# Second block's prelude: the compression weights in the idle half of h, position rows between weight loads, and other orders on four engines

## The chip, the cores and the metric

The kernel is one program on one core of a Trainium2 chip. The metric is the device time of one launch in microseconds. The time before is 1586.78 us, the median of three runs (1584.68 to 1588.28).

## The reference, cut to what matters

The program computes four layers over 256 latent and 256 context tokens (width 1024), and then one block of another kind over the 256 latent tokens. The change lies where the second begins. There, `h` is the normed latent activation and `w_in` one wide projection. Only its first mixer has the compression:

```python
h = rms_norm(x, norm_mix[l])
cols = split_columns(h @ w_in[l])          # a_q a_kc a_vc a_ks a_vs a_kw a_vw a_gate b_* c_* merge
def compress(z, which):                    # z = a_kc or a_vc, windows of 32 tokens, stride 16: 15 of them
    blk = z[:, :, win_idx] + cmp_pos[which]
    hid = jax.nn.gelu(blk.reshape(b, G, n_cmp, CMP_LEN * HEAD_DIM) @ cmp_w1[which])
    return hid @ cmp_w2[which]
k_cmp = rms_norm(compress(kc, 0), k_g)
v_cmp = compress(vc, 1)
bias_c = jnp.transpose(tab[t5_bucket(dist_c)], (2, 3, 0, 1))     # relative position bias, 16 heads
logits_c = jnp.einsum('bgrtd,bgnd->bgrtn', q, k_cmp) * scale + bias_c
```

`cmp_w1` is two matrices of 2048 x 256. The three attention branches (compressed, selected and windowed in the first mixer, one band in the second, a causal one with forgetting in the third) make 80 score units of 128 queries each. A merge and a gated MLP follow.

## The kernel before, in words

Everything is FP32. A product with a weight is done as three fp32r matmuls: ScalarE copies a raw piece of 128 x 512 into a high part (`act_cast`, `s_whi`), VectorE makes the rest (`dve_cast`, `s_wlo`), TensorE multiplies high by high, low by high and high by low. The activation is held in two such halves too, `Hh` and `Hl`, each [128, 8, 512]: columns 0 to 255 are the context's, 256 to 511 the latent tokens'. After the fourth layer's keys and values nobody reads the context's columns again.

SyncE loads the weights in the order of one list of jobs (`plan`, `sp_loads`), 512 KB a chunk, into a ring of four chunks (`s_raw`). A chunk waits until the chunk four before it is cast (or, for weights used raw in FP32, multiplied). SyncE's queue is in order, so a waiting load holds all behind it. The jobs of `cmp_w1` are ("w1", which, half), two chunks each. They are used raw: `pe_hid` multiplies a half by the windows `ST` in 8 small matmuls, and both halves sum up in bank 1. The result goes through `act_hid` part 0 (a copy into the tile `OS`), `pe_hid_sum` (a matmul with a selection matrix), `act_hid` part 1 (GELU into `HID`) and `pe_hid_out`. For the keys (`which` 0) come a norm (`v_hid_k`, a square on ScalarE, `v_hid_mean`, `POOL`, `v_hid_n`), a transpose (`pe_hid_turn`) and the scaled copy `KC`, which the first score unit needs. The values end in `VM`.

The position bias is 16 strips of 128 KB, read from a small DRAM tensor `ext_rows` with overlapping rows, one DMA a head.

The order of work in the second block is written out by hand, one function an engine: `pe_second`, `act_second`, `v_second`, `sp_all`. The prelude does the first six products of 256 columns (`pe_product_2` with keys 512, 768, 1024, 0, 256, 1816, each for two blocks of tokens i = 0, 1), the head norms and turns, and the compression. A head's norm is `act_take` (bank to `NQ` in `s_X`), `act_head_sq`, `v_head_mean`, a power on GpSimd, `v_head_n`, `pe_head_turn` and `act_head_ev`. Then 86 slots follow. A slot of TensorE has about two chunks (three matmuls each) of the remaining products, a transpose of probabilities (`pe_prob`) of the unit four slots before, and one score. VectorE's slot s has the row maximum of unit s - 1 (`v_row_max_2`), the normalisation of unit s - 3 and up to two casts. Up to unit 8 a score also waits for the row maximum of the unit before it.

Of the kernel before, what the change touches and what calls it, by code (L numbers as in the profile page):

```python
# [237 lines left out]
def plan_2():  # L238
# [21 lines left out]

def plan():
# [108 lines left out]
class Weights:  # L370


    def __init__(self, jobs, dram, areas, hi, lo, placed, spent):
# [11 lines left out]
        for j in jobs:  # L385
# [43 lines left out]
class Net:  # L429

    def __init__(self, nc, ctx, ins, out):
        self.nc, self.ins, self.out = nc, ins, out
# [37 lines left out]
        self.w = Weights(jobs, ins["weights"], {0: raw, 1: self.SF[:, 0:8192], 2: GF[:, :]}, hi, lo, placed, self.spent)  # L470
        self.cast = {"act": 0, "dve": 0}

# [2420 lines left out]
    def pe_hid_sum(self, pe, w):  # L2893
        pe.wait_ge("hid_a", (1, 5)[w])
# [3 lines left out]
        for q in range(2):  # L2898
            mk = pe.matmul(self.ps[w][:, 64 * q:64 * q + 64], self.tile_2("OS")[:, 128 * q:128 * q + 128], self.tile_2("selC"), start=True, stop=True)
# [45 lines left out]
    def pe_second(self, pe):  # L2945
# [32 lines left out]
        self.pe_hid_sum(pe, 1)  # L2978
# [916 lines left out]
```

## Time and profile before

| | us |
|---|---|
| median of three runs | 1586.78 |
| the profiled execution | 1587.17 |
| its span | 1585.4 |
| TensorE busy | 1512.4 |
| VectorE busy | 1009.7 |
| ScalarE busy | 808.1 |
| idle of TensorE in 1100 to 1120 us | 5.07 |

The profiled execution lasted 1.8 us longer than its span (what lies around the first and last instruction). The prelude that the change rewrites runs from about 1060 to 1113 us, the slots from there to about 1280 us. A timeline row is: start, length (both us), engine, line, operation, destination and source, shapes, count of instructions merged, and in brackets the idle time before it and what ended it. A `x16` row of `s_raw,s_X` is one `pe_hid` (each FP32 matmul is recorded as two).

### The profile page before, as it was taken

The numbers are of one execution on the slowest core, as the hardware profiler recorded it, in microseconds if no ns is written. First come the engines' busy times: TensorE is split into PE (matmuls) and PEld (weight loads), VectorE is DVE, ScalarE is ACT, GpSimd is POOL, SyncE is SP. The second block draws the span as 40 slices with busy tenths as digits, with TensorE's granted clock in tenths as the row PEclk, the third lists the DMA queues.
The fourth block names the chain that finished last, engine by engine and source line by source line (L and its number), as shares of the span: only waits on it lengthen the run. The fifth ranks groups of instructions, "written<-read, shape, count | busy, mean of one in ns | idle before, by whom it ended". The sixth has DMA issues, their size and how long they took to land.

```text
span 1585.4 us, 28886 instructions
## 1 busy us (share of the span) xinstructions
PE 1512.4 (95%) x11163; PEld 1310.3 (83%) x11163; DVE 1009.7 (64%) x2579; ACT 808.1 (51%) x1956; POOL 110.4 (7%) x220
## 2 busy tenths in 40 slices
PE   6999999999999988999999999888999999999998
PEld 4777779977889967888999888787777799999997
DVE  3687775655555555676676699665566565566655
ACT  3565664544444444333334566655666444465543
POOL 1011110100000110010001111001101000000000
PEclk9999999999999999999999999999999999999999
DMA  9543322334322322232222442237322245555563
GB/s 362 222 121 108 99 76 88 150 103 128 113 93 90 130 94 93 92 111 104 94 94 81 176 119 83 78 120 244 116 79 62 77 130 177 173 186 160 197 198 111
DMA packets 59963, 203.41 MB, mean 128 GB/s; under 512 B 7731, under 2 KB 10499, under 8 KB 59826
## 3 DMA queue, kind: packets, MB, share of 16 engines
q1 hardware_dynamic: 58081, 197.08, 36.5%
q0 software_dynamic: 1600, 4.28, 1.4%
q8 instruction: 89, 1.46, 0.4%
q14 instruction: 49, 0.39, 0.1%
q10 hardware_dynamic: 144, 0.20, 0.0%
HBM read 200.43 MB, written 1.07 MB: 127 GB/s over the span
## 4 chain that ended last, share of the span: by engine, by line
PE 78%; DVE 11%; ACT 4%; issue 3%; DMA 2%; SPq 1%; POOL 1%; DVEq 0%; ACTq 0%
PE ps L48 74%; PE ps L51 5%; DVE s_wlo L57 2%; ACT SF L54 2%; DVE SF L60 1%; DVE SF L66 1%; SPq L87 1%; DVE SF L57 1%; DVE s_SR L57 1%; DVE SF L75 1%; ACT s_whi L54 1%; DMA s_raw<-in_weights_dram 1%; DMA SF<-in_weights_dram 1%; DMA SF<-in_mlmask_dram 1%; DVE s_G L57 1%
## 5 line engine op out<-in xcount | busy, mean ns | idle before, releaser
L57 DVE TENSOR_TENSOR s_wlo<-s_raw,s_whi 128x512 fp32r<-128x512 f32 (+1 forms) x490 | 317.0, 682 | 120.4 <-ACT s_whi L54 119.2
L48 PE MATMUL ps<-s_Hh,s_whi 128*128 128x256 f32 (+2 forms) x992 | 324.0, 327 | 8.9 <-DVE s_Hl L57 8.0
L48 PE MATMUL ps<-s_Hh,s_wlo 128*128 128x256 f32 (+2 forms) x992 | 312.7, 315 | 0.0
L48 PE MATMUL ps<-s_Hl,s_whi 128*128 128x256 f32 (+2 forms) x992 | 312.5, 315 | 0.0
L54 ACT ACTIVATE s_whi<-s_raw 128x512 fp32r<-128x512 f32 (+1 forms) x490 | 281.5, 620 | 54.5 <-PE ps L48 50.0
L54 ACT ACTIVATE SF<-ps 128x512 f32<-128x512 f32 (+3 forms) x328 | 146.6, 463 | 259.8 <-PE ps L51 170.8
L48 PEld LDWEIGHTS ps<-s_Hh,s_whi 128*128 128x128 f32 (+1 forms) x992 | 188.4, 190 | 36.2 <-issue 16.9
L48 PE MATMUL ps<-s_whi,s_Hh 128*128 128x256 f32 (+1 forms) x688 | 209.0, 304 | 6.2 <-DVE s_wlo L57 5.5
L48 PEld LDWEIGHTS ps<-s_Hh,s_wlo 128*128 128x128 f32 (+1 forms) x992 | 188.7, 190 | 13.1
L48 PE MATMUL ps<-SF 128*64 128x128 f32 (+6 forms) x1368 | 192.4, 313 | 6.5 <-DVE SF L60 4.2
L48 PEld LDWEIGHTS ps<-s_Hl,s_whi 128*128 128x128 f32 (+1 forms) x992 | 189.0, 190 | 10.7
L48 PE MATMUL ps<-s_wlo,s_Hh 128*128 128x256 f32 (+1 forms) x688 | 195.4, 284 | 0.0
L48 PE MATMUL ps<-s_whi,s_Hl 128*128 128x256 f32 (+1 forms) x688 | 195.3, 284 | 0.0
L48 PEld LDWEIGHTS ps<-SF 128*64 128x64 f32 (+2 forms) x1368 | 125.3, 158 | 56.4 <-issue 36.9
L48 PEld LDWEIGHTS ps<-s_whi,s_Hh 128*128 128x128 f32 x688 | 132.7, 193 | 17.7 <-issue 8.5
L51 PE MATMUL ps<-s_K,SF 128*128 128x128 f32 (+5 forms) x780 | 128.1, 276 | 17.7 <-DVE SF L60 7.4
L48 PEld LDWEIGHTS ps<-s_wlo,s_Hh 128*128 128x128 f32 x688 | 132.8, 193 | 0.8
L48 PEld LDWEIGHTS ps<-s_whi,s_Hl 128*128 128x128 f32 x688 | 132.6, 193 | 0.0
L54 ACT ACTIVATE SF<-SF,s_st 128x513 f32<-128x513 f32 (+5 forms) x208 | 115.2, 554 | 21.0 <-DVE s_st L75 14.5
L51 PEld LDWEIGHTS ps<-s_K,SF 128*128 128x128 f32 (+5 forms) x780 | 93.3, 142 | 31.8 <-DVE SF L60 11.0
L57 POOL TENSOR_TENSOR s_st<-s_st,s_mhalf 128x1 f32<-128x1 f32 (+4 forms) x58 | 55.7, 961 | 785.2 <-DVE s_st L60 785.1
L48 PE MATMUL ps<-s_whi,s_Gh 128*128 128x256 f32 x336 | 99.0, 295 | 7.8 <-DVE s_Gl L57 6.1
(198 smaller groups left out, 2571.2 us busy)
## 6 DMA issues: line engine op xcount, KB each, us to landing
s_raw<-in_weights_dram SPq DMA_DIRECT2D x308, 512.0 KB, 4.1
GF<-in_weights_dram SPq DMA_DIRECT2D x32, 512.0 KB, 9.0
SF<-in_weights_dram SPq DMA_DIRECT2D x16, 512.0 KB, 13.3
s_raw<-in_weights_dram SPq DMA_DIRECT2D x6, 384.0 KB, 3.4
s_gp<-in_l_g_post_dram POOLq DMA_DIRECT2D x16, 128.0 KB, 3.8
s_bg<-in_l_b_ada_dram POOLq DMA_DIRECT2D x16, 128.0 KB, 4.5
SF<-ext_rows SPq DMA_DIRECT2D x16, 128.0 KB, 3.1
s_X<-in_ctx_dram SPq DMA_DIRECT2D x2, 512.0 KB, 5.2
```

The source lines that it names most:

```text
L48: return self.e.matmul(*a, **k)
L51: return self.e.transpose(*a, **k)
L54: return self.e.activation(*a, **k)
L57: return self.e.tensor_tensor(*a, **k)
L60: return self.e.tensor_scalar(*a, **k)
L66: return self.e.scalar_tensor_tensor(*a, **k)
L75: return self.e.tensor_tensor_reduce(*a, **k)
L87: return self.e.dma_start(*a, **k)
```

## The change

The four `w1` jobs no longer go through the ring. They have a place of their own, `HF`, an FP32 view of the context's columns of `Hh` and `Hl`. Those of the keys stand in the load list ahead of the fourth layer's `w_out`; those of the values come into the same places once the keys' halves are multiplied. Half of the 16 strips are loaded with a load between every two, the other half after the first row maximum. On TensorE, ScalarE and VectorE the steps stand in another order, and the values' `OS` has a tile of its own, `OS1`.

```diff
+        lone = {("w1", w, h): self.w1_place(w, h) for w in range(2) for h in range(2)}
+    def w1_place(self, w, h):
+        tile = self.HF[:, h]
+        free = ("v_mm", V_AT[3] + 2) if w == 0 else ("w1", h + 1)
+        return lambda c: (tile[:, c.k0:c.k1, 0:256], f"area{4 * h + c.k0 // 4}", 3 + w, free)
...
-    jobs = [p(512), p(768), p(1024), small, p(0), w1(0, 0), p(256), w1(0, 1), w1(1, 0), p(1816), w1(1, 1)]
+    jobs = [p(512), p(768), p(1024), small, p(0), p(256), p(1816), w1(1, 0), w1(1, 1)]
...
-        jobs += mix(l) + [job(("out", l, j), f"l{l}_w_out", 256 * j, 256) for j in range(4)]
+        jobs += mix(l) + (first_w1() if l == 3 else []) + [job(("out", l, j), f"l{l}_w_out", 256 * j, 256) for j in range(4)]
@@ def pe_second
         self.pe_hid(pe, 0, 0)
+        self.pe_hid(pe, 0, 1)
         self.pe_head_turn(pe, 0)
         pe.wait_ge("p_ev", 2)
         self.pe_product_2(pe, ("p", 256), 4, 0, range(8), 6)
         self.pe_small_sums(pe)
         self.pe_head_turn(pe, 1)
-        self.pe_hid(pe, 0, 1)
+        self.pe_hid_sum(pe, 0)
         self.pe_product_2(pe, ("p", 256), 4, 1, range(8), 6)
-        self.pe_hid_sum(pe, 0)
+        self.pe_hid(pe, 1, 0)
+        self.pe_hid_out(pe, 0)
         self.pe_head_turn(pe, 2)
-        self.pe_hid(pe, 1, 0)
         pe.wait_ge("p_ev", 4)
         self.pe_product_2(pe, ("p", 1816), 5, 0, range(8), 7)
-        self.pe_hid_out(pe, 0)
+        self.pe_hid(pe, 1, 1)
         self.pe_head_turn(pe, 3)
-        self.pe_hid(pe, 1, 1)
         self.pe_product_2(pe, ("p", 1816), 5, 1, range(8), 7)
+        self.pe_hid_sum(pe, 1)
         self.pe_hid_turn(pe)
-        self.pe_hid_sum(pe, 1)
@@ def act_second
         self.act_take(act, 0, 7)
+        self.act_hid(act, 0, 0)
         self.act_head_ev(act, 0)
         self.act_head_sq(act, 2)
         self.act_head_ev(act, 1)
-        self.act_hid(act, 0, 0)
+        self.act_hid(act, 0, 1)
+        self.act_take(act, 256, 6)
+        self.act_cast(act, w.first(("p", 1816)) + 2)
+        self.act_head_sq(act, 3)
         cast(("p", 1816))
-        self.act_take(act, 256, 6)
-        self.act_hid(act, 0, 1)
-        self.act_head_sq(act, 3)
         self.act_head_ev(act, 2)
+        self.act_hid(act, 1, 0)
@@ def v_second
         cast(("p", 1304))
+        v.wait_ge("ld_strip", 128)
         self.v_head_mean(v, 4)
+        self.v_row_max_2(v, 0)
         self.v_head_n(v, 4)
-        v.wait_ge("ld_strip", 256)
...
-            self.dve_cast(v, self.castable(at, at + 2, **self.slot_done(slot)))
+            if slot > 1:
+                self.dve_cast(v, self.castable(at, at + 2 + 2 * (slot < 4), **self.slot_done(slot)))
@@ def sp_all
-        self.sp_loads(sp, self.load_at(("p", 0)))
+        self.sp_loads(sp, self.load_at(("p", 1816)))
         sp.wait_ge("st_ext", 16)
         sp.wait_ge("turned", 40)
         sp.wait_ge("p_mm", 1)
         for h in range(16):
+            if h == 8:
+                self.sp_loads(sp, self.load_at(("p", ORDER_2[3])))
+                sp.wait_ge("row_max", UNIT_AT[4] + 1)
             src = bass.AP(ext.tensor, ext.offset + 384 * h + 1, [[1, 128], [1, 256]])
             sp.dma_start(self.F(7424, 16, 256)[:, h, :], src).then_inc(S["ld_strip"], 16)
+            if h % 2 == 1:
+                self.sp_loads(sp, self.loaded + 1)
```

SyncE's queue from the first step of the prelude. `SF<-ext_rows` is a strip, `HF` a `w1` chunk, `s_raw` a chunk of the ring; before the change:

```order
L87 DMA s_raw<-in_weights_dram 128x1024 x6
L87 DMA s_raw<-in_weights_dram 128x256
L87 DMA s_raw<-in_weights_dram 128x1024 x2
L87 DMA SF<-ext_rows 128x256 x16
L87 DMA s_raw<-in_weights_dram 128x1024 x138
```

and with it:

```order
L87 DMA s_raw<-in_weights_dram 128x1024 x6
L87 DMA s_raw<-in_weights_dram 128x256
L87 DMA s_raw<-in_weights_dram 128x1024 x6
L87 DMA SF<-ext_rows 128x256 x2
L87 DMA HF<-in_weights_dram 128x4x256
L87 DMA SF<-ext_rows 128x256 x2
L87 DMA HF<-in_weights_dram 128x4x256
L87 DMA SF<-ext_rows 128x256 x2
L87 DMA HF<-in_weights_dram 128x4x256
L87 DMA SF<-ext_rows 128x256 x2
L87 DMA HF<-in_weights_dram 128x4x256
L87 DMA s_raw<-in_weights_dram 128x1024 x8
```

The chunks of products 256 and 1816 now stand ahead of the strips; the values' `w1` stands between them.

ScalarE in the middle of the prelude: `s_X<-ps` is `act_take`, `s_gp<-ps` the copy into `OS`, `s_CS<-ps` the GELU, `s_whi<-s_raw` casts of 1816. Before:

```order
L54 ACTIVATE SF<-ps,s_VC 128x512
L54 ACTIVATE s_gp<-ps 128x256
L54 ACTIVATE s_whi<-s_raw 128x512 x4
L54 ACTIVATE s_X<-ps 128x512
L54 ACT_TABLE_LOAD
L54 ACTIVATE s_CS<-ps 128x128
L54 ACTIVATE SF<-s_X 128x512
L54 ACTIVATE SF<-ps,s_VC 128x512
```

and with the change:

```order
L54 ACTIVATE SF<-ps,s_VC 128x512
L54 ACT_TABLE_LOAD
L54 ACTIVATE s_CS<-ps 128x128
L54 ACTIVATE s_X<-ps 128x512
L54 ACTIVATE s_whi<-s_raw 128x512 x2
L54 ACTIVATE SF<-s_X 128x512
L54 ACTIVATE s_whi<-s_raw 128x512 x2
L54 ACTIVATE SF<-ps,s_VC 128x512
```

The GELU and its table now stand ahead of product 256's take and of the casts, and the square of head 3 (`SF<-s_X`) between the second and the third cast.

VectorE where the slots begin (`L75` is a row maximum, `s_G` head 4's norm, `s_wlo` casts of product 1560):

```order
+L75 ISA SF,s_st<-ps,SF 128x7
+L75 ISA s_st 128x1
 L57 TENSOR_TENSOR s_G<-s_X,s_st 128x4x64 x2
-L57 TENSOR_TENSOR s_wlo<-s_raw,s_whi 128x512 x2
 L75 ISA SF,s_st<-ps,SF 128x7
 L75 ISA s_st 128x1
-L57 TENSOR_TENSOR s_wlo<-s_raw,s_whi 128x512 x2
-L75 ISA SF,s_st<-ps,SF 128x7
-L75 ISA s_st 128x1
+L57 TENSOR_TENSOR s_wlo<-s_raw,s_whi 128x512 x4
```

The first row maximum stands ahead of head 4's norm, and the four casts between the second and the third maximum instead of two and two from the start.

## Rows read from the trace of the kernel before

**Rows 1.** Windows of 20 us: busy us (count) by engine, PE clock, DMA share, GB/s.
```profile
1080.00:1100.00 20.00, 18.22 (x168) 14.79 (x167) 9.22 (x23) 11.44 (x21) 2.65 (x2) 1.00 0.73 258
1100.00:1120.00 20.00, 14.93 (x97) 11.84 (x97) 10.07 (x31) 10.49 (x26) 3.33 (x3) 0.76 0.63 227
1120.00:1140.00 20.00, 20.00 (x135) 15.52 (x135) 11.49 (x51) 10.98 (x38) 2.01 (x1) 0.99 0.17 54
```

**Rows 2.** Timeline of TensorE, its waits and marks from 1082 to 1123 us.
```profile
1082.09 1.40 PE L48 MATMUL ps<-s_raw,s_X 128*32 128x256 f32 x16
...
1085.56 0.35 PE L48 MATMUL ps<-s_Gh,s_Hh 128*128 128x256 f32 x1 [1.48 <-DVE s_Gl L57]
...
1103.83 1.11 PE L51 MATMUL ps<-s_K,s_X 128*128 128x128 f32 x4 [3.24 <-DVE s_X L57]
...
1111.61 0.66 PE L48 MATMUL ps<-s_K,s_gp 128*128 128x64 f32 x4 [1.43 <-ACT s_gp L54]
...
1112.96 0.38 PE L48 MATMUL ps<-s_band,SF 64*128 64x7 f32 x2
...
1114.96 0.59 PE L48 MATMUL ps<-s_band,SF 64*128 64x7 f32 x2 [0.40 <-DVE s_st L75]
...
1122.47 0.27 PE L51 MATMUL ps<-s_K,SF 128*7 128x128 f32 x1
```

**Rows 3.** Timelines of ScalarE, VectorE and GpSimd, 1079 to 1115 us.
```profile
1079.14 0.21 ACT L54 ACTIVATE adaF<-ps 128x48 f32<-128x48 f32 x1 [2.14 <-PE ps L51]
...
1084.06 2.39 ACT L54 ACTIVATE s_Gh<-s_raw 128x512 fp32r<-128x512 f32 x4 [4.71 <-DMA s_raw<-in_weights_dram]
...
1098.32 1.28 ACT L54 ACT_TABLE_LOAD   x1
1099.61 0.28 ACT L54 ACTIVATE s_CS<-ps 128x128 f32<-128x128 f32 x1
...
1101.41 1.64 POOL L57 TENSOR_TENSOR s_st<-s_st,s_mhalf 128x8 f32<-128x8 f32 x1 [8.37 <-DVE s_st L60]
...
1103.08 0.69 DVE L57 TENSOR_TENSOR s_X<-s_X,s_st 128x512 f32<-128x512 f32 x1 [1.57 <-POOL s_st L57]
...
1113.53 1.29 DVE L57 TENSOR_TENSOR s_wlo<-s_raw,s_whi 128x512 fp32r<-128x512 f32 x2
```

**Rows 4.** Windows of 1 us in which the granted clock changes, columns as in rows 1.
```profile
1103.00:1104.00 1.00, 0.17 (x1) 0.17 (x2) 0.89 (x3) 0.00 (x0) 0.05 (x1) 0.75 0.53 213
...
1106.00:1107.00 1.00, 1.00 (x9) 0.26 (x2) 0.78 (x2) 1.00 (x3) 0.00 (x0) 0.54 0.00 0
...
1113.00:1114.00 1.00, 1.00 (x8) 0.98 (x8) 1.00 (x3) 1.00 (x3) 0.00 (x0) 0.87 0.65 266
...
1120.00:1121.00 1.00, 1.00 (x7) 0.86 (x6) 0.00 (x0) 0.61 (x1) 0.00 (x0) 0.72 0.08 20
```

**Rows 5.** Timeline of TensorE: how long the pieces last at either clock.
```profile
1088.38 0.28 PE L48 MATMUL ps<-s_Gh,s_Hl 128*128 128x256 f32 x1
...
1090.18 0.66 PE L51 MATMUL ps<-s_K,s_G 128*128 128x128 f32 x4
1090.77 1.07 PE L48 MATMUL ps<-s_raw,s_X 128*32 128x256 f32 x16
...
1099.95 0.63 PE L48 MATMUL ps<-s_gp,s_CS 128*32 128x64 f32 x8
...
1104.87 1.94 PE L48 MATMUL ps<-s_raw,s_X 128*32 128x256 f32 x16
...
1115.48 1.06 PE L48 MATMUL ps<-s_gp,s_CS 128*32 128x64 f32 x8
```

**Rows 6.** Who PE waited for, 1121 to 1282 us: total us, times, longest.
```profile
PE ps L51 <- DVE SF L60: 0.8, 2, 0.5
```

**Rows 7.** Windows of 1 us: strips alone in flight, then weight chunks alone.
```profile
1074.00:1075.00 1.00, 1.00 (x11) 0.95 (x10) 0.29 (x4) 0.00 (x0) 0.80 (x1) 1.00 0.93 256
...
1080.00:1081.00 1.00, 1.00 (x11) 1.00 (x10) 0.74 (x5) 0.00 (x0) 0.00 (x0) 1.00 0.99 406
```

More of the change, by code:

```diff
@@ L130, in raw @@
         c = self.chunk(k)
+        if len(c.raw.shape) == 3:
+            return c.raw[:, k - c.k0, :]
         return c.raw[:, (k - c.k0) * self.w:(k - c.k0 + 1) * self.w]
@@ L258, in plan_2, with w1, first_w1 @@
     return jobs
+def w1(w, h):
+    return Job(("w1", w, h), [(0, "cmp_w1_2", (0, w), 1024 * h, 0, 256)], 8, 256, False)
+def first_w1():
+    return [w1(0, 0), w1(0, 1)]
 def plan():
@@ L390, in __init__ @@
             for c in j.chunks:
+                if j.key in lone:
+                    c.raw, c.sem, c.nth, c.before = lone[j.key](c)
+                    cols = (c.k1 - c.k0) * j.w
+                    c.off, off = off, off + 128 * cols
+                    c.src = dram[c.off:off].rearrange("(p k c) -> p k c", p=128, c=j.w)
+                    continue
                 mine, n = rings[j.ring], areas[j.ring].shape[1] // CHUNK
@@ L434, in __init__ @@
         self.X = sb("X", [128, 4, D])
+        with nc.sbuf_tensor("HF", [128, 2, 8, 512], F32) as self.HF:
+            pass
         self.Hh, self.Hl = sb("Hh", [128, 8, 512], R32), sb("Hl", [128, 8, 512], R32)
@@ L469, in __init__ @@
         self.ada_last = {j.key: n + 1 for n, j in enumerate(j for j in jobs if j.key[0] == "ada")}
[L470 removed]
+        lone = {("w1", w, h): self.w1_place(w, h) for w in range(2) for h in range(2)}
+        self.w = Weights(jobs, ins["weights"], {0: raw, 1: self.SF[:, 0:8192], 2: GF[:, :]}, hi, lo, placed, lone, self.spent)
         self.cast = {"act": 0, "dve": 0}
+    def w1_place(self, w, h):
+        tile = self.HF[:, h]
+        free = ("v_mm", V_AT[3] + 2) if w == 0 else ("w1", h + 1)
+        return lambda c: (tile[:, c.k0:c.k1, 0:256], f"area{4 * h + c.k0 // 4}", 3 + w, free)
     def F(self, at, *shape):
@@ L2761, in tile_2 @@
             return a[:, at:at + (48 if name == "GS" else 16)].rearrange("p (i g) -> p i g", i=2)
+        if name == "OS1":
+            return self.bg[:, 0, :]
         if name in ("OS", "W2"):
@@ L2898, in pe_hid_sum @@
         for q in range(2):
-            mk = pe.matmul(self.ps[w][:, 64 * q:64 * q + 64], self.tile_2("OS")[:, 128 * q:128 * q + 128], self.tile_2("selC"), start=True, stop=True)
+            mk = pe.matmul(self.ps[w][:, 64 * q:64 * q + 64], self.tile_2("OS" if w == 0 else "OS1")[:, 128 * q:128 * q + 128], self.tile_2("selC"), start=True, stop=True)
         mk.then_inc(self.S["hid_pe"], 1)
@@ L3253, in act_hid @@
             if w == 1:
-                act.wait_ge("hid_v", 2)
-            act.activation(self.tile_2("OS"), self.ps[1][:, 0:256], ACT.Copy).then_inc(S["hid_a"], 1)
+                act.wait_ge("gate_g", 16)
+            act.activation(self.tile_2("OS" if w == 0 else "OS1"), self.ps[1][:, 0:256], ACT.Copy).then_inc(S["hid_a"], 1)
         else:
-            act.wait_ge("hid_pe", 1 if w == 0 else 4)
+            act.wait_ge("hid_pe", 1 if w == 0 else 3)
             act.activation(self.tile_2("HID"), self.ps[w][:, 0:128].rearrange("p (c m) -> p c m", c=2), ACT.Gelu_apprx_tanh).then_inc(S["hid_a"], 1)
@@ L3550, in v_second @@
         self.v_head_n(v, 3)
-        mean = self.v_hid_mean(v)
-        self.v_hid_n(v, mean)
+        self.v_hid_n(v, self.v_hid_mean(v))
         cast(("p", 1304))
+        v.wait_ge("ld_strip", 128)
         self.v_head_mean(v, 4)
+        self.v_row_max_2(v, 0)
         self.v_head_n(v, 4)
-        v.wait_ge("ld_strip", 256)
         for slot in range(SLOTS_2 + 1):
             u = slot - 1
-            if 0 <= u < 80:
+            if 0 < u < 80:
                 self.v_row_max_2(v, u)
@@ L3592, in v_row_max_2 @@
             mask = strip[:, 8 * br + h, 128 - 128 * i:256]
+        if br == 1:
+            v.wait_ge("ld_strip", 256)
         if u > 3:
```

16 lines of the change are left out of this document (7 added, 9 removed).

## The prediction

> **What bounds the kernel now.** I first read the windows of 20 us. TensorE is busy for nearly all of 1120 to 1140 us, but only 14.93 us of the 20 between 1100 and 1120, where its granted clock is 0.76 as well, and 18.22 between 1080 and 1100 [rows 1]. Then TensorE's timeline through the prelude. It has three long waits: 1.48 us for VectorE's cast of product 256, 3.24 us for head 2's norm, 1.43 us for the values' copy `OS`, and 0.40 us at the second score [rows 2]. Third, the other engines, to see what lies behind those waits. ScalarE casts product 256 only at 1084.06, after 4.71 us for a weight DMA [rows 3]; that chunk is queued behind all 16 strips. Fourth, the list of waits in the slots: the largest entry there is 0.8 us in 160 us [rows 6], so from the first slot on TensorE's own work sets the pace, and what it gains before them reaches the end. Last, the windows of 1 us for the clock.
>
> **What the old stretch consists of.** My marks are the first `pe_hid` at 1082.09, the first score at 1112.96 and the first transpose of probabilities at 1122.47 [rows 2]; the change alters nothing on TensorE outside them.
> From 1082.09 to 1112.96 are 30.87 us. The waits are 1.48 + 3.24 + 1.43 = 6.15, and 0.33 more in the first `pe_hid`, which takes 1.40 where one undisturbed takes 1.07 [rows 2, 5]. Two very small waits of about 0.2 each I leave in. In the windows of 1 us the clock is at half (1.2 instead of 2.4 GHz) from about 1103.5 to 1106.9: 0.75 in the first window means a half of it slow, 0.54 in the last 0.92 [rows 4]. What ran there is four transposes (1.11 against 0.66), a `pe_hid` (1.94 against 1.07) [rows 2, 5]: 0.45 + 0.87 = 1.3 us. Work at full clock: 30.87 - 6.15 - 0.33 - 1.3 = 23.1, and without the two small waits 22.7.
> From 1112.96 to 1122.47 are 9.51 us. One wait of 0.40; the clock is at half again from about 1113.74 to 1120.56 [rows 4]. `pe_hid_out` takes 1.06 there against 0.63, the transposes 0.45 more. An estimate for the rest: half of the remaining 4 or 5 us that run slow. I take 2.8 in all. Work at full clock 6.3.
>
> **Removed and moved on SyncE.** With the change the six loads up to product 1816 stand ahead of the strips. The chunks of 256 wait only for casts of earlier products, so they land well before ScalarE, free at 1079.35 [rows 3], wants them; it casts them until 1081.8 and VectorE until 1083.4. The 1.48 is gone; next after it is nothing until head 0's turn. The keys' `w1` is loaded 100 us earlier, so 0.33 goes too. Those four chunks (2 MB) come ahead of the fourth layer's `w_out`. The DMA queues are idle more than half of the time there, and the ring is four chunks deep, so I cost them at nothing; if that cover were gone, each of the four would hold `w_out` by 2 us.
> Now the new wait: the values' first `w1` chunk waits in SyncE's queue until TensorE has multiplied the keys' first half, at 1083.2 by the walk below. Behind it are six strips, three `w1` chunks and product 1304's two chunks, 3.93 MB. Chunks into `HF` are cut in pieces of 1 KB a row, as the strips are. Strips alone moved 256 GB/s, ring chunks alone 406 [rows 7]. I take the strips' rate for `HF`: 2.88 MB / 0.256 = 11.3 us, then 1.05 / 0.406 = 2.6, and about 1.5 until the last has landed: 1098.6. ScalarE wants 1304 at 1100.1. It fits, by little. The Trainium skill, DMA: Bandwidth & Descriptors, Specifications, says that pieces of 512 B and more reach the line rate. The rows here speak against it for 1 KB pieces (256 against 406). By the page these loads would land by 1094.5 and the rival on them below would have no chance; the sum stays as it is.
>
> **The walk with the new orders**, each step by the lengths above (product 2.94 a block, from 1085.56 to 1088.38 and 0.12 [rows 2, 5]). TensorE: two `pe_hid` to 1084.2, turn of head 0 1084.8, product 256 block 0 1087.8, small sums 1089.3, turn 1 1089.9, `pe_hid_sum` 1090.3, block 1 1093.2, `pe_hid` of the values 1094.3, `pe_hid_out` 1094.9. Turn 2 needs head 2's norm. Its square is no more behind four casts, a take and a table load: done 1086.4, mean, power 1.64 and multiply 0.69 [rows 3] give 1090.4. So the 3.24 is gone. Turn 2 ends at 1095.5.
> Product 1816 needs its casts. ScalarE: table load 1.28 and GELU from 1090.4 to 1092.1, take of 256 at 1093.2 (it waits for TensorE), two casts to 1094.9, square of head 3, two casts to 1096.6. VectorE's first low part is ready at 1095.1, each next in time. Block 0 ends at 1098.4, second `pe_hid` of the values at 1099.5. Turn 3 is what comes late next: VectorE has all four low parts at 1097.3, then the mean (0.9), the power (1.64) and the multiply (0.69): 1100.6. A new wait of 1.1 us stands here. Behind it on TensorE: the block 1 of 1816, and with it everything.
> Turn 3 to 1101.2, block 1 to 1104.1, `pe_hid_sum` and `pe_hid_turn` to 1104.8, two chunks to 1105.5. `KC` is ready at 1105.1 (the copy `OS1` is made at 1099.8 in a tile of its own, so the 1.43 goes). The first score stands at 1105.5. By the other sum, 1082.09 + 22.7 + 1.1 = 1105.9. I take 1105.7: 7.3 us earlier.
> The Trainium skill, ScalarE: Activation LUTs, What ACT_TABLE_LOAD costs, adds a drain of 1.38 us to each load of 1.28. The rows show the load of 1.28 with the GELU 0.01 us behind it [rows 3], so the sum has no drain. By the page the casts of 1816 would come 1.4 us later and TensorE would wait about 1 us more.
>
> **At the start of the slots.** The 0.40 goes, since the first row maximum now stands ahead of head 4's norm. But four casts (2 x 1.29 [rows 3]) stand ahead of the third row maximum, for which score 3 waits: VectorE does row maximum 1 at 1108.4, the casts to 1110.9, row maximum 2 to 1111.2, and TensorE is there at 1110.2. A new wait of 1.0. The slow clock before was preceded by 3.24 + 1.43 us without work and a time of small instructions; with waits of 1.1 and 1.0 I expect full speed. Gain 2.8 + 0.4 - 1.0 = 2.2.
>
> **Sum.** 7.3 + 2.2 = 9.5, and as all the many handovers are taken without slack, I take off 0.3: 9.2 us. From the profiled execution, 1587.17 - 9.2 = 1578.0; the median of three is 0.4 below that execution, so 1577.6. What happens from the first transpose on is unchanged, except half of the strips, which come with 30 to 70 us to spare before unit 48.
> Bounds: the clock's 4.1 us (1.3 + 2.8) may not come back at all, which leaves 5.1. On the good side, the two new waits (2.1) may be shorter or hidden, and the later slow spells in the slots may vanish: 12 at most.
>
> **The rivals.** *A slow spell stays.* TensorE still does many small FP32 matmuls and transposes and has two waits. Then 2.8 to 4.1 are missing: 1581. For it: the spell at 1113.7 came only 1.43 us of wait after 7 us at full clock [rows 2, 4]. Against: that stretch had two waits, the new one has the same sum in smaller parts. *Loads come late.* At 200 GB/s for `HF` and strips, the last lands at 1101.7, at 160 at 1105.3, 5.2 us after ScalarE wants it; ScalarE has 1.2 to spare, so 4.0 lost: 1581.6. *The stall only moves.* If the turns and norms, not the loads, are what TensorE really waits for, the 3.24 comes back at turn 3: 9.2 - 3 - 2 (its slow clock) gives 1582. *Slower.* SyncE's queue behind the keys' `w1`: if pieces of 1 KB of weights move at 100 GB/s (4 times as many descriptors as a ring chunk), 28.8 + 2.6 + 2 us bring 1304 to 1116.6, 16.5 after it is wanted, 15.3 of them on the path: 1577.6 + 15.3 = 1593. It decides below about 130 GB/s, where 9.2 + 1.2 us of delay are used up. The strips at 256 speak against it. *It doesn't do what it says:* if the slots, not the prelude, set the end, 1586.8. Rows 6 speak against it.
>
> **How the numbers follow.** Forecast 57% (its own range 1575 to 1580); slow spell 17%; loads late 7%; the stall moves 8%; no change 6%; slower 5%. The range to 1583 holds the first four cases and down to 1574 the better end. No change means within 0.2%, 3.2 us, about what this measurement can tell. Faster by more: 57 + 17 + 7 + 6 of the 8 = 0.87; same 0.08; slower 0.05.
>
> **What would show it.** In the profile after: product 256 without a wait; no wait over 0.5 at turn 2; a wait of about 1 at turn 3 and at score 3; the first score near 1105.7 and the first transpose of probabilities near 1113; clock 1.00 from 1100 to 1120; SyncE's issues of the values' `w1` at 1083 and later. I am wrong if ScalarE waits for a DMA at product 1304, if the clock has a spell of 0.5 there, or if the distance from the first transpose to the end is more than 1 us longer than before (462.9 us to the end of the span, 1585.4 - 1122.47).

## The result, and the profile after

The change makes the kernel faster: 1578.58 us, the median of seven runs (1574.91 to 1581.33), against 1586.51 (1583.12 to 1594.13) for the kernel before on the same chip. The ratio is 0.9942, with a 95% interval of 0.9923 to 0.9961, so 9.2 us with an interval of 6.2 to 12.2. Forecast were 1577.6 us and 9.2 us. The profiled execution of after lasted 1574.91 us (span 1573.1). It is the fastest of the seven, so its 12.3 us below the profiled one of before say too much.

The windows of 20 us of after, columns as in [rows 1]:

```profile
1080.00:1100.00 20.00, 18.84 (x191) 15.87 (x190) 10.67 (x28) 12.59 (x25) 4.28 (x3) 1.00 0.77 247
1100.00:1120.00 20.00, 19.61 (x144) 16.52 (x143) 12.54 (x49) 13.94 (x41) 1.69 (x2) 1.00 0.37 123
```

The second window is the one to compare: 19.61 us of TensorE at full clock, where before it was 14.93 at 0.76. The timeline of TensorE after answers to [rows 2]:

```profile
1081.88 1.93 PE L48 MATMUL ps<-HF,s_X 128*32 128x256 f32 x32
...
1084.15 0.36 PE L48 MATMUL ps<-s_Gh,s_Hh 128*128 128x256 f32 x1
...
1093.85 0.66 PE L51 MATMUL ps<-s_K,s_X 128*128 128x128 f32 x4
...
1099.82 0.66 PE L51 MATMUL ps<-s_K,s_X 128*128 128x128 f32 x4 [1.16 <-DVE s_X L57]
...
1104.82 0.38 PE L48 MATMUL ps<-s_band,SF 64*128 64x7 f32 x2
...
1109.99 0.48 PE L48 MATMUL ps<-SF 64*128 64x128 f32 x2 [0.39 <-DVE s_st L75]
...
1111.58 0.27 PE L51 MATMUL ps<-s_K,SF 128*7 128x128 f32 x1
```

From the top: both `pe_hid` of the keys in one piece, product 256 without a wait, turn 2 without a wait, turn 3 with 1.16, the first score, score 3 with 0.39, the first transpose of probabilities. Of 6.55 us of waits at four places, 1.55 at two places are left. The turn behind the 3.24 of before was turn 3 as well, not turn 2 as the prediction has it (below). The engines behind the waits, after, as in [rows 3]:

```profile
1079.03 2.18 ACT L54 ACTIVATE s_Gh<-s_raw 128x512 fp32r<-128x512 f32 x4
...
1089.91 1.28 ACT L54 ACT_TABLE_LOAD   x1
1091.21 0.28 ACT L54 ACTIVATE s_CS<-ps 128x128 f32<-128x128 f32 x1
...
1097.41 1.64 POOL L57 TENSOR_TENSOR s_st<-s_st,s_mhalf 128x8 f32<-128x8 f32 x1 [8.63 <-DVE s_st L60]
...
1107.24 2.49 DVE L57 TENSOR_TENSOR s_wlo<-s_raw,s_whi 128x512 fp32r<-128x512 f32 x4
```

ScalarE casts product 256 as soon as it is free, with no DMA wait in front (before 4.71). The power for head 3 runs from 1097.41, after all of VectorE's casts of 1816; that makes the 1.16. The four casts at 1107.24 make the 0.39. Two of the windows of 1 us, in which [rows 4] had 0.54 and 0.87:

```profile
1106.00:1107.00 1.00, 1.00 (x12) 0.86 (x11) 0.52 (x2) 0.98 (x3) 0.44 (x1) 1.00 0.97 360
...
1113.00:1114.00 1.00, 1.00 (x8) 0.67 (x6) 0.32 (x2) 0.65 (x3) 0.00 (x0) 1.00 0.79 247
```

All windows from 1096 to 1126 us show 1.00. Last, the waits of TensorE in the slots after, 1111 to 1274 us, which answer to [rows 6]:

```profile
PE ps L51 <- DVE SF L60: 0.8, 2, 0.5
PE ps L51 <- ACT SF L54: 0.3, 1, 0.3
```

**How the traces are compared.** The executions reach the first `pe_hid` between 1079.8 and 1087.3 us, whatever the kernel. So I count from there to the first score and to the first transpose of probabilities ("transpose" below). Each row of the table is one profiled execution. Half clock is the time at 1.2 instead of 2.4 GHz between 1080 and 1125 us, summed from windows of 1 us (a window at 0.75 counts as a half). The ratio is to the kernel before on the same chip.

| kernel | waits of TensorE, us | first score | transpose | half clock | ratio (95%) |
|---|---|---|---|---|---|
| before | 1.48, 3.24, 1.43, 0.40 | 30.87 | 40.38 | 3.4 + 6.8 | 1 |
| after | 1.16, 0.39 | 22.94 | 29.70 | 0 | 0.9942 (0.9923 to 0.9961) |
| after again, `c_after` | 1.15, 0.39 | 22.94 | 29.71 | 0 | 0.9918 (0.9892 to 0.9944) |
| `e1_old_pe_act` | 0.97, 1.44 | 24.70 | 33.94 | 6.8 | 0.9958 (0.9927 to 0.9989) |
| `e2_old_sp` | 1.15, 0.39 | 22.94 | 29.71 | 0 | 0.9915 (0.9883 to 0.9947) |
| `e3_shared_os` | 1.15, 1.29 | 24.35 | 35.05 | 10.2 | 0.9960 (0.9936 to 0.9985) |
| `e4_old_dve` | 1.16, 2.48 | 22.93 | 34.72 | 6.8 | 0.9965 (0.9938 to 0.9991) |
| `e5_delay` | 2.21, 0.39 | 24.00 | 30.77 | 0 | 0.9926 (0.9902 to 0.9951) |
| `e6_mean_early` | 0.25 | 22.17 | 28.48 | 0 | 0.9901 (0.9872 to 0.9930) |
| `e7_both` | 0.24 | 22.17 | 28.48 | 0 | 0.9910 (0.9884 to 0.9936) |
| `e8_keys_w1_late` | 1.15, 0.39 | 22.95 | 29.72 | 0 | 0.9940 (0.9918 to 0.9961) |
| `e9_delay_at_turn` | 0.25, 1.54, 0.38 | 24.19 | 33.40 | 6.8 | 0.9963 (0.9938 to 0.9989) |
| `e10_long_delay` | 4.20, 0.39 | 27.50 | 34.27 | 3.4 | 0.9955 (0.9937 to 0.9973) |
| `e11_os1_alone` | 1.20, 3.24, 1.02, 1.11 | 30.09 | 37.59 | 3.4 | 0.9988 (0.9971 to 1.0005) |

The distances repeat to 0.02 us where nothing is altered (after, `c_after`, `e2`, `e8`), while the intervals of the ratios are some 5 to 10 us wide. Steps of 1 us are read from the distances, and the ratio only tells that they reach the end. Where they are larger, the times bear them out: `e1` to `e4` ran on one chip, and the medians of `e1`, `e3` and `e4` lie 6.0, 4.6 and 5.0 us above that of `e2`, whose transpose stands where after's does; by the transposes it is 4.2, 5.3 and 5.0. No execution of `e3` or `e4` was as fast as the slowest of `e2`.

### The profile page after: what moved, and what is told of

Its sections match the earlier page's. It is cut to its first block, busy times and chain, and to the rows that moved or that the text cites. A ratio compares the mean times of both kernels' runs of the same rounds, so it can differ in the third digit from the quotient of the medians.

```text
span 1573.1 us, 28886 instructions
## 1 busy us (share of the span) xinstructions
PE 1505.4 (96%) x11163; PEld 1306.8 (83%) x11163; DVE 1008.6 (64%) x2579; ACT 807.7 (51%) x1956; POOL 110.2 (7%) x220
## 4 chain that ended last, share of the span: by engine, by line
PE 80%; DVE 11%; ACT 4%; issue 3%; DMA 1%; SPq 1%; POOL 1%; DVEq 0%; ACTq 0%
PE ps L48 75%; PE ps L51 5%; DVE s_wlo L57 2%; ACT SF L54 2%; DVE SF L60 1%; DVE SF L66 1%; DVE SF L57 1%; DVE s_SR L57 1%; DVE SF L75 1%; ACT s_whi L54 1%; DMA SF<-in_weights_dram 1%; DMA SF<-in_mlmask_dram 1%; SPq L87 1%; DVE s_G L57 1%; POOL s_st L57 1%
## 5 line engine op out<-in xcount | busy, mean ns | idle before, releaser
L48 PEld LDWEIGHTS ps<-s_Hl,s_whi 128*128 128x128 f32 (+1 forms) x992 | 188.5, 190 | 10.7
```

Of the source, the lines that this page charges most:

```text
L48: return self.e.matmul(*a, **k)
```

## The experiments

### Undoing one part at a time

**The orders of TensorE and ScalarE.** `e1` has the new loads and VectorE's new order, with the old `pe_second` and `act_second` and the shared `OS`. (It also undoes two exchanges on ScalarE that no run undoes alone: the casts of product 1304 ahead of head 3's copy, and `KC` ahead of head 4's square.)

```diff
-        self.pe_hid(pe, 0, 1)
         self.pe_head_turn(pe, 0)
...
+        self.pe_hid_turn(pe)
         self.pe_hid_sum(pe, 1)
-        self.pe_hid_turn(pe)
...
-        self.act_hid(act, 0, 0)
         self.act_head_ev(act, 0)
```

> The changed kernel with TensorE's and ScalarE's orders and the shared OS tile of before; loads (HF, strips) and VectorE's slots stay as changed. Theory A (the waits of before came from late weight loads, first of all): with the loads alone there is no wait at product 256, none at turn 2, about 0.5 us at turn 3, and the wait of about 1.4 us for the values' copy stays; first score near 1106.2 (changed kernel 1104.8, before 1113.0), clock full from 1100 to 1120, time about 1.4 us above the changed kernel's. Theory B (the orders of TensorE and ScalarE are worth as much as the loads): a wait of 2 us or more comes back at turn 2 or 3, first score at 1108.5 or later, time 4 us or more above the changed kernel's.

Measured: 1581.74 us (1576.6 to 1595.3). The wait of 1.48 does not come back, and where 3.24 stood there are 0.97, so the new orders of TensorE and ScalarE are not needed to shorten those two. What comes back is the wait for the values' copy and a stretch at half clock. Theory A was right on which waits stay (0.5 forecast at turn 3) and nearly on the first score (24.3 us after the first `pe_hid`), and wrong on the clock and so on the time. TensorE's timeline, and two windows, of `e1`:

```profile
1103.37 0.66 PE L51 MATMUL ps<-s_K,s_X 128*128 128x128 f32 x4 [0.97 <-DVE s_X L57]
...
1109.77 0.66 PE L48 MATMUL ps<-s_K,s_gp 128*128 128x64 f32 x4 [1.44 <-ACT s_gp L54]
```

```profile
1112.00:1113.00 1.00, 1.00 (x6) 0.79 (x4) 0.40 (x2) 0.98 (x3) 0.00 (x0) 0.50 0.00 0
...
1117.00:1118.00 1.00, 1.00 (x6) 1.00 (x7) 0.79 (x5) 0.51 (x3) 0.00 (x0) 0.50 0.89 320
```

**SyncE's order.** `e2` has all 16 strips ahead of product 256 again, and the values' `w1` behind them.

```diff
-        self.sp_loads(sp, self.load_at(("p", 1816)))
+        self.sp_loads(sp, self.load_at(("p", 0)))
...
-            if h == 8:
-                self.sp_loads(sp, self.load_at(("p", ORDER_2[3])))
-                sp.wait_ge("row_max", UNIT_AT[4] + 1)
...
-            if h % 2 == 1:
-                self.sp_loads(sp, self.loaded + 1)
```

> The changed kernel with SyncE's order of before in the prelude: all 16 strips in one go after product 0's chunks, then products 256 and 1816, then the values' w1 into HF. The keys' w1 stays early. Theory A: ScalarE waits about 4.7 us for product 256's chunk as before, TensorE waits 1.0 to 1.5 us at product 256; the rest of the new orders absorbs the delay (ScalarE's square of head 2 comes at about 1090.5, ahead of where turn 2 needs it), so first score near 1106.5, time about 2 us above the changed kernel's. Theory B (SyncE's order is the whole gain): the 3.2 us wait at turn 2 or 3 is back and a slow spell with it, first score near 1111, time 8 us above the changed kernel's.

Measured: 1575.78 us (1573.95 to 1577.3), distances equal to after's. ScalarE's timeline in `e2`:

```profile
1084.04 2.44 ACT L54 ACTIVATE s_Gh<-s_raw 128x512 fp32r<-128x512 f32 x4 [2.43 <-DMA s_raw<-in_weights_dram]
```

ScalarE waits 2.43 us for product 256's chunk, which lands 0.3 us ahead of the first `pe_hid` (before 2.0 behind it, since two chunks of the keys' `w1` were queued ahead of it too), and TensorE does not wait at all, since its two `pe_hid` (1.93 us) and the turn of head 0 lie ahead. Both theories fell. With the keys' `w1` out of the way, the strips' place is worth nothing.

**The keys' early `w1`**, the counterpart: `e8` loads it in the prelude, still into its own place.

```diff
-        jobs += mix(l) + (first_w1() if l == 3 else []) + [job(...)]
+        jobs += mix(l) + [job(...)]
...
-    jobs = [..., small, p(0), p(256), p(1816), w1(1, 0), w1(1, 1)]
+    jobs = [..., small, p(0), w1(0, 0), p(256), w1(0, 1), p(1816), w1(1, 0), w1(1, 1)]
```

> The changed kernel, but the keys' four w1 chunks are loaded in the prelude (the first half between products 0 and 256, the second between 256 and 1816), still into their own place, not the ring. All else as with the change. Theory (the early load of the keys' w1 is what takes the wait for product 256 away: 2 MB more now stand in SyncE's queue near it, and moved 400 GB/s they take 5 us): ScalarE's casts of 256 come up to 5 us later, TensorE waits 0.5 to 2 us at product 256 or at the first pe_hid; if that is all, the total is 1 to 2 us over the changed kernel. Rival (with the strips behind 1816 the queue has slack, so this too is worth nothing, like SyncE's order): the same as the changed kernel within 0.5 us. Second rival (the wait also brings a stretch at half clock): 4 to 6 us over.

Measured: 1576.95 us (1571.79 to 1580.22), again after's distances. ScalarE's cast of product 256 in `e8` has no wait for a DMA:

```profile
1084.42 2.18 ACT L54 ACTIVATE s_Gh<-s_raw 128x512 fp32r<-128x512 f32 x4
```

The rival held. The keys' `w1` ahead and the strips behind do the same job, and one of the two is enough. The two were not undone together with the rest kept. That the loads suffice for the 1.48 is shown by `e1`, where the old orders of TensorE and ScalarE stand with the new loads and product 256 has no wait. No run has the new orders with the old loads, so what the orders would save by themselves there, and at turn 3, is open.

**The values' own tile.** `e3` puts the copy back into the shared `OS`, behind `KC`.

```diff
-        self.pe_hid_sum(pe, 1)
         self.pe_hid_turn(pe)
+        self.pe_hid_sum(pe, 1)
...
-        self.act_hid(act, 1, 0)
...
+        self.act_hid(act, 1, 0)
         self.act_hid(act, 1, 1)
```

> The changed kernel with the values' copy again in the keys' OS tile, so after the keys' norm: the copy stands last of ScalarE's prelude and the selection matmul after the keys' turn. Theory A: TensorE waits 1.2 to 1.5 us between the keys' turn and that matmul, first score near 1106.2, time 1.4 us above the changed kernel's, and no slow spell. Rival: the wait brings the slow clock back within 5 us, as it did before, and costs 3 us more (4.5 in all).

Measured: 1580.33 us (1578.23 to 1583.47). TensorE's timeline and a window of `e3`:

```profile
1103.23 0.66 PE L48 MATMUL ps<-s_K,s_gp 128*128 128x64 f32 x4 [1.29 <-ACT s_gp L54]
```

```profile
1105.00:1106.00 1.00, 1.00 (x5) 1.00 (x5) 0.85 (x4) 1.00 (x3) 0.00 (x0) 0.50 0.79 311
```

The wait costs 1.41 us at the first score. From there to the transpose it takes 10.70 instead of 6.76, although after's wait of 0.39 is not there: 3.94 + 0.39 = 4.3 for the half clock. The rival was right in kind, with 4.3 where it had 3. `e1` undoes this part as well, and its transpose comes at 33.94, ahead of the 35.05 here. So beside `OS1` the new orders of TensorE and ScalarE bring 0.35 us at the first score (24.70 against 24.35) and nothing at the transpose; the 4.2 of `e1` is mostly the values' copy and the clock behind it.

**VectorE's order at the slots.** `e4` has head 4's multiply ahead of the first row maximum, and two casts in every slot from the first.

```diff
         self.v_head_mean(v, 4)
-        self.v_row_max_2(v, 0)
         self.v_head_n(v, 4)
...
-            if slot > 1:
-                self.dve_cast(v, self.castable(at, at + 2 + 2 * (slot < 4), ...))
+            self.dve_cast(v, self.castable(at, at + 2, ...))
```

> The changed kernel with VectorE's order of before where the slots begin: head 4's norm and two casts ahead of the first row maximum, two casts more ahead of the second. First score unchanged at 1104.8. Theory A: the first row maximum ends at 1108.6, so score 1 waits 2.5 us for it (0.39 at score 3 goes), first transpose of probabilities near 1113.7 instead of 1111.6, time 2 us above the changed kernel's. Rival: VectorE's order is hidden (before, the wait there was 0.40), time the same.

Measured: 1580.73 us (1578.85 to 1587.92). TensorE's timeline and a window of `e4`:

```profile
1110.72 0.39 PE L48 MATMUL ps<-s_band,SF 64*128 64x7 f32 x2 [2.48 <-DVE s_st L75]
```

```profile
1113.00:1114.00 1.00, 1.00 (x5) 0.55 (x4) 0.00 (x0) 0.00 (x0) 0.00 (x0) 0.50 0.75 287
```

From the first score to the transpose 11.79 us instead of 6.76: 5.03, of which 2.09 (2.48 - 0.39) are waits and 2.94 the half clock. Theory A had the wait (2.5) and not the clock.

### One part alone

`e11` is the kernel before with `OS1`, its early copy and the two steps of TensorE exchanged.

```diff
-        self.pe_hid_turn(pe)
         self.pe_hid_sum(pe, 1)
+        self.pe_hid_turn(pe)
...
+        self.act_hid(act, 1, 0)
         self.act_head_sq(act, 4)
-        act.wait_ge("hid_pe", 3)
+        act.wait_ge("hid_pe", 4)
...
-        self.act_hid(act, 1, 0)
```

> The kernel before with one part of the change alone: the values' copy has the tile OS1 and is made ahead of head 4's square, and pe_hid_sum of the values stands ahead of pe_hid_turn. The 1.43 us wait goes; the waits of 1.48 at product 256 and 3.24 at turn 2 stay. Theory (this wait and the clock's second fall behind it belong together): first score 1.4 earlier (29.4 us after the first pe_hid), first transpose of probabilities 1.4 + 2.8 earlier (36.2), total 4 us under the kernel before. Rival (the second fall came from the 3.24 us and the small matmuls before it): 1.4 us under, at 39.0. Second rival (the copy now stands ahead of head 4's square or KC and delays the first score): no gain.

Measured: 1585.69 us (1582.14 to 1589.42), 1.9 us by the ratio, with an interval that holds 0. TensorE's timeline and windows of `e11`:

```profile
1100.91 0.80 PE L51 MATMUL ps<-s_K,s_X 128*128 128x128 f32 x4 [3.24 <-DVE s_X L57]
...
1108.18 0.66 PE L48 MATMUL ps<-s_K,s_bg 128*128 128x64 f32 x4 [1.02 <-ACT s_bg L54]
...
1112.31 0.39 PE L48 MATMUL ps<-s_band,SF 64*128 64x7 f32 x2 [1.11 <-DVE s_st L75]
```

```profile
1102.00:1103.00 1.00, 1.00 (x16) 0.40 (x8) 0.74 (x5) 1.00 (x3) 0.00 (x0) 0.50 0.00 0
...
1113.00:1114.00 1.00, 1.00 (x11) 0.87 (x8) 0.54 (x3) 0.77 (x4) 0.00 (x0) 1.00 0.71 164
```

The theory was half right. The clock's second fall is gone, and from the first score to the transpose it takes 7.50 instead of 9.51, although a wait there is 0.71 longer: 2.7 us for that fall. But 1.02 of the 1.43 stays (`OS1` is ready late in the old order of ScalarE), and the gain goes into a new wait of 1.11 for a row maximum. The first fall, behind the 3.24, is untouched.

### What makes the clock fall

The runs above left two ideas: what counts is how long TensorE waits (S, the sum of its waits), or where (P, the place). Three kernels add waits, two of them to after and one to `e6` (below), by memsets of a free bank on VectorE, each waiting for the one before. `c_after` is the measure beside the first.

> The changed kernel itself, unaltered, as the measure for the three kernels beside it on this chip. Expected: 1578.6 us as before, ratio to the kernel before 0.994, within 0.15%; first score 22.9 us and first transpose of probabilities 29.7 us after the first pe_hid; no stretch at half clock between 1080 and 1125 us.

Measured: 1575.26 us (1571.28 to 1577.89). The distances came as expected, to 0.01 us. The ratio, 0.9918, is 0.0024 lower, beyond the 0.15% expected; the two intervals overlap.

```diff
         self.v_hid_k(v)
+        for _ in range(4):      # e5; 7 in e10
+            v.step(v.memset(self.ps[5][:, :], 0.0))
+            v.after()
         self.v_head_n(v, 3)
```

> The changed kernel with four extra memsets of a free bank of PSUM on VectorE, each waiting for the one before (about 0.6 us each, 2.5 in all), ahead of head 3's norm multiply. TensorE's wait at turn 3 then grows from 1.16 to about 3.7 us; nothing else is altered, and the output is the same. Theory (a wait of this length near the stretch of small FP32 matmuls is paid twice, once as the wait and once as a stretch at half clock behind it): a stretch of several us at half clock follows, first transpose of probabilities 29.7 + 2.5 + 3 to 4 = 35 to 36 us after the first pe_hid, total 5.5 to 6.5 us over the changed kernel. Rival (the clock falls for another reason, such as which small matmuls stand there, and a wait costs only its own length): 32.2 us, total 2.5 over, clock 1.00. Second rival (nothing, since VectorE has slack): same as the changed kernel; speaks against it that turn 3 waited for VectorE.

Measured: 1576.34 us (1575.37 to 1578.28), 1.1 over `c_after`. 1.57 us of the 2.67 of memsets lay in VectorE's own wait for GpSimd, so the wait at turn 3 grew by 1.06 only, from 1.15 to 2.21, and that is all it cost (1.06 at the transpose). The theory that a wait is always paid twice fell, for a wait of 2.21 at this place.

> The changed kernel with seven such memsets ahead of head 3's norm multiply instead of four. The wait at turn 3 was 1.16 + 4 x 0.67 - 1.57 = 2.21 (measured) with four, so it will be 4.2 to 4.3 with seven, longer than the 3.24 of the kernel before. Theory S (sum of waits): a stretch at half clock follows, first transpose of probabilities 29.7 + 3.1 + 2 to 4 = 35 to 37 us after the first pe_hid. Theory P (place: big matmuls stand behind this wait, the small ones come 4 us later): clock 1.00, 32.8 us.

Measured: 1580.46 us (1575.45 to 1581.82). TensorE's timeline and windows of `e10`:

```profile
1103.31 0.66 PE L51 MATMUL ps<-s_K,s_X 128*128 128x128 f32 x4 [4.20 <-DVE s_X L57]
```

```profile
1103.00:1104.00 1.00, 0.69 (x6) 0.69 (x7) 0.59 (x3) 0.00 (x0) 0.29 (x1) 0.92 0.00 0
1104.00:1105.00 1.00, 1.00 (x6) 1.00 (x6) 0.57 (x4) 0.69 (x1) 0.39 (x1) 0.50 0.00 0
...
1107.00:1108.00 1.00, 1.00 (x9) 1.00 (x9) 0.56 (x1) 0.00 (x0) 0.00 (x0) 0.87 0.71 115
```

3.05 us of wait more, and 3.4 us at half clock right behind, which cost 4.56 - 3.05 = 1.5. Then full clock again.

`e9` is `e6` (below) with a wait that ends 1.6 us ahead of the first score:

```diff
         v.wait_ge("rs", mean)
+        for _ in range(4):
+            v.step(v.memset(self.ps[5][:, :], 0.0))
+            v.after()
         for g in range(2):
```

> On the better version (head 3's mean early, no wait at turn 3), four memsets of a free bank of PSUM, each waiting for the one before (0.67 us each), stand ahead of the multiply of the compressed keys, so that TensorE waits 1.5 to 1.9 us at pe_hid_turn, 1.1 us before the first score; the output is the same. It tells apart what makes the clock fall. Theory P (place: a wait counts where small FP32 matmuls and the scores with it stand close behind; the run with the late copy had one of 1.29 here): a stretch of 6 to 10 us at half clock behind it, first transpose of probabilities 28.5 + 1.7 + 3 to 5 = 33 to 35 us after the first pe_hid. [...]

Measured: 1579.33 us (1573.33 to 1585.98). TensorE's timeline and windows of `e9`:

```profile
1107.17 0.24 PE L51 MATMUL ps<-s_K,s_band 32*128 32x32 f32 x1 [1.54 <-DVE SF L60]
```

```profile
1107.00:1108.00 1.00, 0.45 (x3) 0.37 (x4) 1.00 (x3) 0.48 (x2) 0.00 (x0) 1.00 0.00 0
...
1110.00:1111.00 1.00, 1.00 (x7) 0.76 (x6) 0.13 (x3) 0.98 (x2) 0.87 (x1) 0.50 0.77 315
...
1116.00:1117.00 1.00, 1.00 (x6) 0.65 (x5) 0.34 (x2) 0.00 (x0) 0.00 (x0) 0.80 0.15 61
```

Waits of 1.54 + 0.38 here bring 6.8 us at half clock (2.9 us of cost: 33.40 - 24.19 against 28.48 - 22.17), where 2.21 at turn 3 brought none. So S, the sum alone, doesn't decide: less wait here did what more did not there. P, the place alone, forecast this but full clock in `e10`, so it fell there. What stands is a table: waits of 3.24 and 4.20 ahead of turn 3 were followed by 3.4 us at half clock; waits of 1.29 to 2.48 shortly ahead of or between the first three scores by 6.8 or 10.2 us; waits of 0.39 to 1.16 anywhere, and of 1.20, 1.48 and 2.21 ahead of turns and blocks of products 256 and 1816, by none. What the throttle counts stays open, and each of these falls, but for the one behind 3.24, was traced in a single execution of its kernel.

### A better version

`e6` takes away the two waits left, on VectorE alone: head 3's mean between the casts of 1816, and two casts in slots 2 and 3.

```diff
-        cast(("p", 1816))
+        self.dve_cast(v, w.first(("p", 1816)) + 2)
         self.v_head_mean(v, 3)
+        cast(("p", 1816))
...
-                self.dve_cast(v, self.castable(at, at + 2 + 2 * (slot < 4), ...))
+                self.dve_cast(v, self.castable(at, at + 2, ...))
```

> Candidate for a better version: on VectorE the mean of head 3 stands between the second and the third low part of product 1816, so that the power on GpSimd runs beside the casts, and in slots 2 and 3 two casts stand instead of four. Theory (the two waits left in the prelude, 1.16 at turn 3 and 0.39 at score 3, are VectorE's order alone): turn 3 waits 0 to 0.4, score 3 not at all, first score 22.0 and first transpose of probabilities 28.5 us after the first pe_hid, 0.8 to 1.5 us under the changed kernel. Rival (the third piece of product 1816 now waits for its low part, which comes 0.3 later): the wait only moves, and the total is the same within 0.3 us.

Measured: 1573.09 us (1569.92 to 1575.7) against 1575.26 for after and 1588.47 for before on the same chip. TensorE's timeline and a window of 20 us of `e6`:

```profile
1095.76 0.39 PE L48 MATMUL ps<-s_whi,s_Hh 128*128 128x256 f32 x1 [0.25 <-DVE s_wlo L57]
```

```profile
1100.00:1120.00 20.00, 20.00 (x142) 16.36 (x142) 14.03 (x54) 15.15 (x46) 1.60 (x3) 1.00 0.41 127
```

Turn 3 and score 3 wait for nothing, a new wait of 0.25 stands at 1816's third piece, and the transpose comes 1.22 us earlier, as the theory said. In the times the 2.2 us between the medians are not beyond doubt, since the intervals of both ratios overlap. `e7` adds `e2`'s order of SyncE:

> As e6, and SyncE in the order before the change (all 16 strips ahead of product 256 and of the values' w1). By the run with the old SyncE order alone (TensorE had no wait by it, median 1575.8 on another chip), theory: the same as e6 within 0.5 us. Rival (fewer loads in flight beside the start of the slots help, or the strips late do): up to 2 us under e6. Second rival (with the shorter turn 3 the loads of product 1304 or 256 now come last): up to 1 us over it.

Measured: 1574.24 us (1571.42 to 1576.54), distances equal to `e6`'s. The theory held: SyncE's order is worth nothing here either.

## Why the prediction was right, point by point

**Total and sum.** 9.2 forecast, 9.2 by the ratio. That the two agree to the tenth is luck: the interval is 6.2 to 12.2, and the same kernel gave 0.9918 as `c_after`, which is 13 us. From the first `pe_hid` to the transpose the two traces differ by 40.38 - 29.70 = 10.7; the sum had 9.5 ahead of the 0.3 taken off.

**Up to the first score**, 7.3 forecast, 7.9 measured. The waits of 1.48 and 1.43 went, and of 3.24 there are 1.16 left, for which the sum had 1.1. The 0.6 left is in the work, which I took a little too slow: 21.8 us (22.94 - 1.16) against 22.3 by the walk and 22.7 by the other sum.

**The wait of 3.24 was put in the wrong place.** The prediction has it at turn 2, for head 2's norm, as a wait that goes, with a new one of 1.1 at turn 3. It is turn 3's: in the timeline of before it stands between `pe_hid_out` (1099.95) and the second `pe_hid` of the values (1104.87) [rows 2, 5], and the order has turn 3 there. So at the turns no wait was removed and none added; one shrank from 3.24 to 1.16. The size came out right because the walk was made for both turns. The cause named, that the head's square no longer stands behind four casts, a take and a table load, was wrong too: in `e1` it stands behind all of them, and 0.97 is left. ScalarE's timeline of before shows what the walk had not carried on:

```profile
1095.41 2.40 ACT L54 ACTIVATE s_whi<-s_raw 128x512 fp32r<-128x512 f32 x4 [3.12 <-DMA s_raw<-in_weights_dram]
...
1099.78 0.62 ACT L54 ACTIVATE SF<-s_X 128x512 f32<-128x512 f32 x1
```

ScalarE waits for a load a second time, 3.12 us at product 1816's casts, and head 3's square is queued behind them. The chain that ends at turn 3 (the view of the critical chain of before, 1090 to 1104 us: start, length, what; `SPq` is SyncE issuing a load) says why the load is late:

```profile
1090.84 1.04 PE ps L48 x16
...
1091.90 0.33 SPq L87
...
1092.27 4.37 DMA s_raw<-in_weights_dram
```

The `x16` is the second `pe_hid` of the keys. Its chunks of `w1` sat in the ring, and product 1816's, four behind them, could not be issued before they were multiplied. Taking `w1` out of the ring ends that, wherever the strips stand (`e2`) and whenever the keys' `w1` is loaded (`e8`). With the new loads the old order leaves 0.97 (`e1`), with the old loads 3.24 stands (`e11`). The rival that the stall only moves had the place right, turn 3, but not its cause: it took the turns and norms for the limit and not the loads, and had the whole 3.24 come back with the slow clock behind it.

**From the first score to the transpose**, 2.2 forecast, 2.75 measured. The term off in size is the new wait at score 3: 0.39, not 1.0. Counted from the first score, VectorE began the four casts at 2.4 us, not 2.7, and had the third row maximum at 5.1, not 5.5, while TensorE came for it at 4.8, not 4.5.

**The clock.** The 2.8 for the second fall measured 2.7 in `e11`, 2.9 in `e9` and `e4`, and 4.3 in `e3`. The 1.3 for the first stands beside 1.5 in `e10`. That waits of 1.1 and 1.0 would leave the clock alone was a guess that held. It was also the closest call: a wait of 1.29 at the wrong place brought the fall back.

**The loads.** Product 256 needs no wait, as forecast, but by either half of the change in the loads. Loading the keys' `w1` early cost nothing visible. The time came out nearly right, the rate behind it not: I let `HF` chunks move like strips, at a steady 256 GB/s. Two windows of after while the values' `w1` and product 1304 are in flight, and the time from issue to landing of 1304's two chunks:

```profile
1084.00:1089.00 5.00, 5.00 (x44) 4.68 (x43) 2.00 (x6) 1.58 (x3) 2.25 (x2) 1.00 0.83 205
1089.00:1096.00 7.00, 6.99 (x70) 6.19 (x69) 2.77 (x6) 5.72 (x10) 0.00 (x0) 1.00 1.09 375
```

```profile
DMA to landing us min/median/max: 7.1/7.4/7.7
```

The two were issued at 1089.35 and 1090.02, so they landed at 1096.5 and 1097.7, and ScalarE wanted them at 1099.21: 1.5 us to spare, where the sum had 1.5 as well (1098.6 against 1100.1). The rate was slower than 256 at first and then faster. The keys' four `HF` chunks moved 254 and 222 GB/s between 972 and 974 us, with hardly anything else in flight, and 368 and 383 between 975 and 977, with a ring chunk queued behind them. The rule of the Trainium skill that I had set aside (DMA: Bandwidth & Descriptors, Specifications: pieces of 512 B and more reach the line rate) agrees with the trace in part: pieces of 1 KB of weights came within a tenth of the 406 of ring chunks, but not all the time, and the landing that followed from it, 1094.5, was further off than the sum's. Why the strips move more slowly was not tried.

**The table load.** The GELU starts 0.02 us after the end of its table load (1089.91 + 1.28, then 1091.21), as the sum had it, and the load starts 0.01 us after the instruction ahead of it. The drain of 1.38 us that the Trainium skill gives (ScalarE: Activation LUTs, What ACT_TABLE_LOAD costs) is not seen here either, so the measurement decides.

**From the transpose to the end**, said not to grow by more than 1: 461.5 after, 462.9 before. The 1.4 less lies in the slots, late. The windows of 60 us, first of before, then of after:

```profile
1240.00:1300.00 60.00, 60.00 (x416) 48.34 (x416) 36.46 (x115) 27.97 (x81) 0.00 (x0) 0.97 0.32 98
```

```profile
1240.00:1300.00 60.00, 60.00 (x451) 51.56 (x449) 36.23 (x97) 29.47 (x76) 0.00 (x0) 1.00 0.35 115
```

TensorE has no idle time in either. Before has a stretch of 3.4 us at half clock there, from about 1257.1 us, with this window in it:

```profile
1258.00:1259.00 1.00, 1.00 (x6) 1.00 (x6) 0.96 (x4) 0.00 (x0) 0.00 (x0) 0.50 0.66 70
```

Counted from the transpose, the timelines of TensorE before and after agree to 0.1 us up to this stretch, come 1.5 us apart in it, and stay so: it is the whole 1.4. No wait stands ahead of it. `e5`, `e10` and `e11` have such a stretch too (0.97 in the same window), the other runs have none, so it does not go with the change alone. What decides it is open.

## What to carry to other kernels

Read the granted clock behind every wait of TensorE: here a wait of 1.3 to 2.5 us beside small FP32 matmuls cost 2.7 to 4.3 us more in half clock, while 2.2 us ahead of a block of large ones cost only itself. So gains of such edits don't add up. Undoing any of three parts gave back 4.2, 5.3 or 5.0 of the 10.7 us at the transpose (`e1`, `e3`, `e4`; the first contains the second), and one of them alone brought 2.8 (`e11`). And when an edit moves loads and engine orders together, undo each by itself: two of the changes in the loads did the same job at product 256. A ring holds a later load back until an earlier chunk is used: ask which use that is before you put a chunk of another kind into it.

## What the runs showed that I had not expected

The clock's falls between 1080 and 1125 us lasted 3.4, 6.8 or 10.2 us, in every kernel that had one, and one more of 3.4 us at about 1257 us came with no wait ahead of it. A wait of 1.29 us brought one back, and 2.21 us elsewhere brought none. A strip of 128 KB with overlapping rows moves at 256 GB/s [rows 7], while 1 KB pieces of weights reach 383 at best. And the distance between two marks of one kernel repeats to 0.02 us from run to run, while the whole time of one kernel spreads over 3 to 19 us: where the marks enclose the change, the trace tells steps apart that the times can't.
